# An RWKV-7 chunk inverse in a hybrid decoder: the masked copies of all levels made ahead on GpSimd

## The reference

```python
def step(S, inp):
    r_t, d_t, k_t, v_t, kk_t, b_t = inp
    sa = jnp.einsum('bhij,bhj->bhi', S, -kk_t)
    S = S * d_t[:, :, None, :] + sa[..., None] * b_t[:, :, None, :] + v_t[..., None] * k_t[:, :, None, :]
    return S, jnp.einsum('bhij,bhj->bhi', S, r_t)

xs = tuple(jnp.moveaxis(t, 1, 0) for t in (r_h, d_h, k_h, v_h, kk, b_h))
S, y = lax.scan(step, s0.astype(f32), xs)
```

## Time and profile before

| | |
|---|---|
| median of 3 runs | 3473.19 us (3470.27 to 3475.51) |
| the profiled execution | 3477.72 us, of it 3475.9 us from the first to the last instruction (the span) |
| mean granted TensorE clock | 0.972 of full speed |
| TensorE, VectorE, ScalarE, GpSimd busy | 94%, 50%, 34%, 4% of the span |
| the six rounds | from 335 to 458 us and from 2048 to 2170 us |

### The profile page before, as it was taken

How to read it: one execution, slowest core, us unless ns; L and a number is a source line. 1 busy time by engine, 2 the same in 40 slices (tenths; PEclk the granted TensorE clock), 3 DMA queues, 4 the chain that set the end, 5 groups by cost and what they waited for, 6 DMA issues and landing times.

```text
span 3475.9 us, 60862 instructions
## 1 busy us (share of the span) xinstructions
PE 3273.6 (94%) x24966; PEld 3067.3 (88%) x24966; DVE 1720.7 (50%) x2267; ACT 1192.1 (34%) x1573; POOL 128.5 (4%) x233
## 2 busy tenths in 40 slices
PE   7997888899999999999999978787999999999998
PEld 7996755499999999999999957455999999999998
DVE  4436673255555454454543366713555544544544
ACT  3224136433232232232432241654333222223224
POOL 2001021000000000000000011200000000000000
PEclk9998989999999999999999988899999999999999
DMA  6660025765554554555565500466655555555554
GB/s 185 160 146 25 2 86 195 271 143 149 147 153 136 158 154 136 159 153 137 142 170 160 123 2 2 156 232 202 146 155 147 145 142 160 145 141 161 141 146 131
DMA packets 846387, 490.47 MB, mean 141 GB/s; under 512 B 96352, under 2 KB 822896, under 8 KB 845808
## 3 DMA queue, kind: packets, MB, share of 16 engines
q1 hardware_dynamic: 845804, 488.53, 50.5%
q10 hardware_dynamic: 452, 0.11, 0.0%
HBM read 480.46 MB, written 8.12 MB: 141 GB/s over the span
## 4 chain that ended last, share of the span: by engine, by line
PE 87%; DVE 6%; ACT 3%; issue 2%; DMA 1%; SPq 0%; ACTq 0%; DVEq 0%
PE PS L1309 83%; PE PS L1310 4%; ACT ktr L819 1%; DMA cV<-in_cache_a_v 1%; ACT psm L790 0%; DVE psm L1182 0%; DVE xm L1024 0%; DVE wl L896 0%; DVE hl L1247 0%; ACT ppt L801 0%; DVE nm L1184 0%; ACT xm L706 0%; DMA sink<-in_c_sink 0%; DVE dK L1063 0%; ACT wh L619 0%
## 5 line engine op out<-in xcount | busy, mean ns | idle before, releaser
L619 ACT ACTIVATE wh<-raw 128x2048 fp32r<-128x2048 f32 (+1 forms) x408 | 711.7, 1744 | 1287.4 <-PE PS L1309 1238.6
L896 DVE TENSOR_TENSOR wl<-raw,wh 128x2048 fp32r<-128x2048 f32 (+1 forms) x408 | 848.8, 2080 | 384.2 <-ACT wh L619 383.7
L1309 PE MATMUL PS<-fh,wh 128*128 128x320 f32 x2816 | 870.6, 309 | 0.0
L1309 PE MATMUL PS<-fh,wl 128*128 128x320 f32 x2816 | 870.1, 309 | 0.0
L1309 PE MATMUL PS<-fl,wh 128*128 128x320 f32 x2816 | 870.1, 309 | 0.0
L1309 PE MATMUL PS<-hh,wh 128*128 128x320 f32 x1664 | 517.7, 311 | 23.6 <-DVE hl L1252 18.3
L1309 PEld LDWEIGHTS PS<-fl,wh 128*128 128x128 f32 x2816 | 528.6, 188 | 0.2
L1309 PEld LDWEIGHTS PS<-fh,wh 128*128 128x128 f32 x2816 | 528.6, 188 | 0.2
L1309 PEld LDWEIGHTS PS<-fh,wl 128*128 128x128 f32 x2816 | 528.6, 188 | 0.0
L1309 PE MATMUL PS<-hl,wh 128*128 128x320 f32 x1664 | 516.4, 310 | 0.0
L1309 PE MATMUL PS<-hh,wl 128*128 128x320 f32 x1664 | 516.2, 310 | 0.0
(11 more groups left out here) (313 smaller groups left out, 2741.9 us busy)
## 6 DMA issues: line engine op xcount, KB each, us to landing
raw<-in_w_gate SPq DMA_DIRECT2D x88, 1024.0 KB, 5.7
raw<-in_w_up SPq DMA_DIRECT2D x88, 1024.0 KB, 5.7
raw<-in_w_down SPq DMA_DIRECT2D x128, 704.0 KB, 4.8
raw<-in_w_in SPq DMA_DIRECT2D x56, 1024.0 KB, 5.6
cK<-in_cache_a_k SPq DMA_DIRECT2D x80, 512.0 KB, 6.3
cV<-in_cache_a_v SPq DMA_DIRECT2D x80, 512.0 KB, 8.2
raw<-in_w_in SPq DMA_DIRECT2D x32, 512.0 KB, 5.8
raw<-in_w_out SPq DMA_DIRECT2D x32, 512.0 KB, 4.5
```

Of the source, the lines that this page charges most:

```text
L619: act.activation(wh[j][:, 0:kts], raw[j][:, 0:kts], ACT.Copy).then_inc(sem["wh"], 1)
L896: tt(wl[j][:, 0:kts], raw[j][:, 0:kts], wh[j][:, 0:kts].bitcast(F32), ALU.subtract).then_inc(sem["wl"], 1)
L1309: mm = lambda out, lhsT, rhs, start=True, stop=True: pe.matmul(out, lhsT, rhs, start=start, stop=stop, skip_group_check=True)
```

## The change

GpSimd makes the masked copies for all levels of a round one after the other, each into a buffer of its own: `corners`, five tiles of which ET is the first (ET4, ET8, ET16, ET32 lie in the region that held S0in, which isn't used any more by then). All of them count on et0. VectorE's `corner` and its wait for Z are gone. TensorE waits for et0 at each level and half where it waited for et, and reads `corners[i]`.

```diff
--- before.py
+++ after.py
@@ -247,6 +247,7 @@
         MT, WT, TT, ET, ZZ, NTm, RBm = (place(n, [P, 512], RS + 2048 * i) for i, n in enumerate(
             ("MT", "WT", "TT", "ET", "ZZ", "NTm", "RBm")))
         tat = place("tat", [P, 512], RS + 28672)
+        corners = [ET] + [place(f"ET{size}", [P, 512], RS + 14336 + 2048 * i) for i, size in enumerate(LEVELS[1:])]
         lora = [place(f"lora{i}", [P, 512], RS + 2048 * i) for i in range(4)]
         S0in = place("S0in", [P, NB, 4, P], RS + 8192)
         ux, vx = ([place(f"{n}{j}", [NS, 2, NB, HD], RS + (12288, 0)[j] + 4096 * i) for j in range(2)] for i, n in enumerate(("ux", "vx")))
@@ -546,10 +547,11 @@
 
                     nt = P if tau < 2 else NS
                     pool.wait_ge(sem["Gc"], 3 * l + tau + 1)
-                    for hf in range(2):
-                        m = C(f"lev{LEVELS[0]}", nt).unsqueeze(1).broadcast_to([nt, 4, HD])
-                        x, y = (z[0:nt, hf * 256:(hf + 1) * 256].rearrange("p (h t) -> p h t", h=4) for z in (MT, ET))
-                        pool.tensor_tensor(y, x, m, ALU.mult).then_inc(sem["et0"], 1)
+                    for size, corner in zip(LEVELS if tau < 2 else LEVELS[:2], corners):
+                        for hf in range(2):
+                            m = C(f"lev{size}", nt).unsqueeze(1).broadcast_to([nt, 4, HD])
+                            x, y = (z[0:nt, hf * 256:(hf + 1) * 256].rearrange("p (h t) -> p h t", h=4) for z in (MT, corner))
+                            pool.tensor_tensor(y, x, m, ALU.mult).then_inc(sem["et0"], 1)
                 pool.wait_ge(sem["G"], 15 * (l + 1))
                 pool.memset(mkb[0][:], 0.0)
                 pool.memset(mkb[1][:], 0.0).then_inc(sem["mz"], 1)
@@ -996,8 +998,6 @@
             def halves():
                 return [slice(0, HD), slice(HD, P)]
 
-            zs = [0]
-
             def rotated(u, part=None):
 
                 n = ROTATED[u].stop - ROTATED[u].start
@@ -1083,19 +1083,8 @@
                     levels = LEVELS if tau < 2 else LEVELS[:2]
                     quad = lambda x, hf: x[0:nt, hf * 256:(hf + 1) * 256].rearrange("p (h t) -> p h t", h=4)
                     qbank = lambda b: PS[0:nt, b, 0:256].rearrange("p (h t) -> p h t", h=4)
-
-                    def corner(size, hf):
-                        m = C(f"lev{size}", nt).unsqueeze(1).broadcast_to([nt, 4, HD])
-                        done(tt(quad(ET, hf), quad(MT, hf), m, ALU.mult), "et")
                     for i, size in enumerate(levels):
                         last = i == len(levels) - 1
-                        if not last:
-                            for hf in range(2):
-                                zs[0] += 1
-                                dve.wait_ge(sem["Z"], zs[0])
-                                corner(levels[i + 1], hf)
-                        else:
-                            zs[0] += 2
                         for hf in range(2):
                             if not last:
                                 take("TZ")
@@ -1473,14 +1462,12 @@
                     for i, size in enumerate(levels):
                         for hf in range(2):
                             hs = range(4 * hf, 4 * hf + 4)
+                            take("et0")
                             if i:
-                                take("et")
                                 take("TT")
-                            else:
-                                take("et0")
-                                if not hf:
-                                    take("E1")
-                            per_head(ZB[hf], ET, TT, hs).then_inc(sem["Z"], 1)
+                            elif not hf:
+                                take("E1")
+                            per_head(ZB[hf], corners[i], TT, hs).then_inc(sem["Z"], 1)
                         for hf in range(2):
                             hs = range(4 * hf, 4 * hf + 4)
                             take("Zc")
```

## The result

The changed kernel takes 3480.51 us in the median of 20 runs (3477.47 to 3486.91), the kernel before 3474.64 (20 runs). The medians differ by 5.9 us. The ratio is 1.0021 with a 95% interval of 1.0015 to 1.0027, which is worth 7.3 us, between 5.2 and 9.4. The forecast was 5.5 us and no change that can be told; it is a small loss that 20 runs can just tell. In the profiled execution the span grew from 3475.9 to 3481.8 us.

The account below looks back on a forecast made before the run. Weight streaming on TensorE fills most of the span; in the inversion, VectorE bounds the opening and TensorE the later levels. Blocking 3.3 us plus lower clock 2.2 us made 5.5 us slower, 3478.7 us, range 3471 to 3487.

Parts of the forecast that it names:

- my forecast: Whole kernel: slower by 2.6 to 6.9 us, likeliest 5.5; chance 0.60.
- The copies leave VectorE and win nothing: Levels: removed VectorE copies worth 0.36 us in each of two rounds, 0.7 us, not gained if the clock falls.
- The opening grows by the blocking: Openings of six rounds: GpSimd's copies and VectorE operations with two SBUF inputs delay each other; 3.3 us slower.
- case A: Opening of four rounds, GpSimd starting 0.61 us before L1073: copy 3 newly delays L1076 by 0.41 us.
- case B: Opening of two rounds, GpSimd starting 0.96 us before L1073: copies 3 and 4 delay L1075 and L1076, 0.82 us.
- Two rounds fall to the lower clock: Level 0 of layer 0, round 1 and layer 1, round 0: longer TensorE wait, clock falls, 1.1 us each, 2.2 us.
- The sign I named: Ahead of the first product with ZZ: TensorE idles about 2.4 us in each of six rounds, if right.
- The sample rounds: Two rounds of sample tokens: no lower-clock loss counted in the sum; two more GpSimd copies there (1.4 us) covered.
- the slow clock lasts longer: Rival, level 0 of all six rounds: 5.6 us more, 11.1 in all, 3484.3 us; chance 0.20.
- No wait takes the place of the one removed: Levels above 0: GpSimd's copies are ready in time, TensorE waits for none; no cost.
- mk is covered: Sample rounds: two more copies (1.4 us) delay GpSimd's clearing of mk, wanted 15 us after the opening; no cost.
- GpSimd keeps its turn: Rival, openings: VectorE's L1073 to L1076 wait for all GpSimd copies; 24 us, 3498 us; chance 0.05.

Follow-up runs that it names:

- e5: Changed kernel plus 24 (sample tokens: 12) unread TensorE products, laid out like the real ones, ahead of the first product with ZZ; 3471.83 us, 0.9996 of the kernel before.
- e8: Changed kernel with GpSimd's copies above level 0 only after RBm, and NTm moved ahead of WT's two operations; 3468.73 us, 0.9986 of the kernel before.
- e1: Changed kernel, but GpSimd waits after its two level 0 copies until VectorE has finished RBm; 3473.24 us, 0.9995 of the kernel before.
- e2: Kernel before, VectorE's copies kept, plus GpSimd's 8 (sample tokens: 2) further copies into tiles nobody reads; 3480.76 us, ratio 1.0017.
- e3: Kernel before, VectorE's copies kept, plus 8 (sample tokens: 2) GpSimd memsets that read nothing; 3473.39 us, ratio 1.0001.
- e6: Kernel before plus one unread VectorE copy of 256 columns out of PSUM in the opening, ahead of NTm; 3476.13 us, ratio 1.0007.
- e7: Kernel before with NTm, which reads PSUM, moved ahead of WT's two operations; 3468.69 us, ratio 0.9987.
- e4: Changed kernel plus 56 unread 64x64 TensorE products, all on one spot, ahead of the first product with ZZ; 3511.96 us, 1.0105 of the kernel before.

## Why the prediction was right, and where its terms were off

The mechanism was right in its main part, the blocking in the opening; the time is in the range, and the loss has the direction and nearly the size forecast: 5.5 against 5.9 us by the medians and 7.3 (5.2 to 9.4) by the ratio, which is a little over the 2.6 to 6.9 that I had called my forecast. That the total comes so near is partly luck: in the profiles the openings cost 0.6 us less than the sum has, the two fallen rounds 0.2 more, and the sample rounds 0.8 where it has nothing. It is on the edge of the 0.2% that I had called the bound: 20 runs of each tell a smaller loss than I had assumed.

1. *The copies leave VectorE and win nothing.* Shown. In the changed kernel TensorE is busy through level 0 in all four rounds. Where the clock held (e5, e8) the gain per round was 0.33 to 0.35 us, against 0.36 predicted.
2. *The opening grows by the blocking.* Shown, by e1, e2 and e3. A case A round grew by 0.39 to 0.42 us (0.41 predicted). **This sum was mis-sized:** 3.3 us predicted, 2.7 measured. The two case B rounds grew by 0.50 and 0.55 instead of 0.82, since in the new trace GpSimd starts behind L1072 in all six rounds, so copy 2 meets L1075 and no longer L1073: two waits of 0.41 us now, where the old round had one of some 0.3. I had taken the case for a property of the round. It is one of the execution: e1, e6 and e7 have it in other rounds (L1073's counterpart at 0.96 to 0.99 us). In the kernel before both case B rounds had made their first Gram products at a low clock (0.56 and 0.55, against 0.75 and 0.98 in the two others), so that L1072 started later against MT.
3. *Two rounds fall to the lower clock.* They did in the profiled execution: 7.58 and 7.57 us for 6.37, 2.4 us against 2.2 predicted; e5 shows that products in the gap bring the 1.00 back. That the longer opening is what brings them down is not shown: e2 and e6 have the longer openings, and two of their four long rounds held. The sign I named, 2.4 us of idleness in each round, came in four of six.
4. *The sample rounds* were costed at nothing and lost 0.8 us to nvs; that was part of a rival ("the slow clock lasts longer"), which for the long rounds did not come: those that had fallen before took 7.60 and 7.60 us for 7.37 and 7.60.
5. *No wait takes the place of the one removed, and mk is covered.* The view of tile ET names nobody who waited for GpSimd, and the updates stay at 0.42 us.
6. *GpSimd keeps its turn* is refuted: ten copies take 8.26 us in layer 0, round 0, and each of VectorE's two waiting operations got in behind the one copy under way (1.10 and 1.09 us).

## What to carry to other kernels

Moving work from VectorE to GpSimd was free here only where VectorE, in that stretch, had no operation with both inputs in SBUF on its path: look for such operations, and put the ones that read PSUM, or GpSimd's memsets, beside GpSimd's reads. Start GpSimd's queue when it is needed and not when it can be: the later start cost nothing here and the early one 0.2%. And price a fraction of a microsecond on TensorE's wait twice, once as itself and once by the clock of what may follow; the granted clock per stretch shows which rounds fell, but one profile is one draw: kernels with the same opening had between two and four fallen rounds. Read a control for its waits as well as for its time: e2 took as long as the changed kernel, in part for another reason.

## What the runs showed of the hardware that was not expected

A 64x64 f32 product laid out over both halves of the partitions, on changing places of the bank, costs 0.058 us each (8 in 0.46 us); on one spot, with one half, 56 of them took 6.48 us at a clock of 1.00, 0.116 us each, twice as much (e4, layer 1), and 10.42 us, 0.19 us each, at a mean clock of 0.58 (layer 0, round 0). So a factor of 2 is the layout, and the rest is the clock; the spot and the half weren't separated.

VectorE's copies, too, have both inputs in SBUF. In e2, which kept them, the two of level 0 took 1.83 us together instead of 0.88 under GpSimd's further copies (layer 0, round 1, at 382.67). In that round TensorE's slower clock hid it (4.57 us for level 0, as in the changed kernel); in the first rounds of the layers it stood on the path and made level 0 4.31 us at 1.00 instead of 3.37.
